# Making the low part of each weight tile one turn later, and moving the last two square-sums of a norm behind the first product of the next opening

## The chip, the cores and the metric

The kernel runs on one core of a Trainium2 chip. The metric is the time on the device, in microseconds (us), as the median of several executions. One execution of the kernel before was also recorded by the hardware profiler, and all rows below come from that one.

## The reference, cut to what matters

Two transformer blocks run one after the other on 512 tokens of width 1024. The first ends in a retrieval layer that picks 16 of 16384 experts for each token and each of 8 heads:

```python
a = jax.nn.gelu(jnp.einsum('tpkd,td->tpk', u[idx], t), approximate=False)
return jnp.einsum('tpk,tpkd->td', (g * a), v[idx])
```

The second block has two layers. Each normalises, mixes (a short convolution or attention, with memory attention beside it), adds, normalises, and runs a gated feed-forward of width 2816:

```python
for i in range(DEPTH_2):
    h = rmsnorm(x, norm_mix[i])
    ...                                   # conv or windowed attention, and memory attention
    x = x + jnp.concatenate([y_tok, y_mem], axis=-1) @ w_out
    h = rmsnorm(x, norm_ffn[i])
    x = x + (jax.nn.silu(h @ w_gate[i]) * (h @ w_up[i])) @ w_down[i]
return rmsnorm(x, final_norm)
```

All of it is float32. The kernel gets that precision from faster matmuls by splitting each operand into a high part and a low part (what the high part leaves over) and adding three products: high by high, low by high, high by low.

## The kernel before, in words

The change touches only the second block. It runs twice, once for each half of the tokens (`half(p, ...)`, p = 0 and 1, 256 tokens each). A half is 184 *products*. A product is one 128-column tile of a weight matrix against the activations: 8 chunks of 128 rows (7 in two thirds of the down projection), and for each chunk three matmuls (`part`, L1813 to L1815). Product n passes through these steps, each in the program of its own engine:

- SyncE loads the raw tile into one of `RAW` = 5 slots once product n-5 is done (`tile`, L1625; it waits for the semaphore `st_used`, which TensorE raises at the end of each product).
- ScalarE copies the high part into one of `SPLIT` = 4 slots once product n-4 is done (`split_hi`, L2150, tile `la_w_hi`; it raises `st_hi`).
- VectorE subtracts the high part from the raw tile and leaves the low part in its place (`split_lo`, L2507, tile `la_w_lo`; it waits for `st_hi` and raises `st_lo`).
- TensorE waits for `st_lo` and for a free PSUM bank (`taken`), and runs the matmuls.
- VectorE, ScalarE or both take the result out of the bank. On VectorE: `scaled` L2520, with `la_work<-la_work` L2609, the product of gate and up, behind each pair of the feed-forward; `add_x` L2527 in the projections back to x. On ScalarE: SiLU L2230, high parts of the hidden L2234, of x L2169, squares L2172. VectorE then makes the low parts: hidden L2594 (`hidden_lo`), x L2512 (`chunk_lo`).

What VectorE does for one product is called a *turn* here. In turn n of the kernel before it takes out product n and then calls `split_lo(n + SPLIT)`.

Each engine's program is a fixed list, and instructions of one engine start in that order. A wait at the head of the list holds everything behind it.

The products of a half come in stages: 20 for the mixing input (the convolution's L2684 to L2693), 8 for `project_out`, 68 for `feed_forward` (22 pairs "in", gate and up, and three groups of 8 "out"), 12 for queries, keys and values, 8 for `project_out`, 68 for `feed_forward`. A stage whose input comes in chunk by chunk begins with an *opening*: three products (`BANKS` = 3) are run on all chunks but the last, and then all three are finished with the last chunk. There are eight openings in a half, among them the last "out" group of each feed-forward.

A norm needs the sum of squares of x over all 8 chunks. ScalarE squares chunk k into one of two slots (L2172, tile `la_sqr`), TensorE adds it up with a matmul by ones (`add_chunk_`, L1849), and after the eighth ScalarE computes the factor `rstd` (`root`, L2159 and L2162). The first five sums stand between the last products of a stage. VectorE needs `rstd` only when it takes out the first product of the next stage.

Beside half 0 the retrieval layer of the first block is still being finished. GpSimd gathers rows of u and v into a ring of 14 slots by indirect DMA (L1694, L1700); VectorE takes dot products of the u rows (`pe_dots`, L2459), TensorE sums the v rows (L1748). The object `beside` spreads this work at some two gathers for each product.

## Time and profile before

| | |
|---|---|
| median of 3 executions | 3271.68 us (3268.64 to 3272.43) |
| the profiled execution | 3267.3 us, of which its span 3265.5 us |
| mean granted clock of TensorE in it | 0.885 of full |
| TensorE matmuls | 2554.1 us busy (78%) |
| VectorE | 1927.5 us (59%) |
| ScalarE | 972.0 us (30%) |
| GpSimd | 1154.3 us (35%) |
| half 0 of the second block, about | 1545 to 2545 us of the span |
| half 1, about | 2545 to 3265 us |

A row of the trace names the engine (PE is TensorE, PEld its weight load, DVE VectorE, ACT ScalarE, POOL GpSimd, SP SyncE), the line, and what is written and read. An arrow `<-` behind an idle time names what ended it. PEclk is the granted clock of TensorE: 1.00 is 2.4 GHz, 0.50 is 1.2 GHz, a value between is a mean over the stretch. The ends of matmuls are modelled, so starts are read and not ends: a matmul shown as 0.28 us long is followed by the next one 0.12 us later.

### The profile page before, as it was taken

To read this page: it belongs to the slowest core of one execution; us is meant where nothing else is said; L and a number is where in the kernel's file an instruction comes from. 1 tells how busy PE (TensorE), PEld (TensorE's weight loads), DVE (VectorE), ACT (ScalarE), POOL (GpSimd) and SP (SyncE) were. 2 spreads that over 40 slices of the span, in tenths; PEclk is the share of its full clock that TensorE was granted. 3 is DMA by queue.
4 is the path that set the end of the run, shared out by engine and by line. 5 is a ranking of instruction groups with operands and counts; after the bars stand their busy time and mean duration, and the time that the engine had idled before them with its cause. 6 is when DMAs were issued, how large, how long until landed. Compare 5 with 4: busy or idle time off the path is not lost.

```text
span 3265.5 us, 43866 instructions
## 1 busy us (share of the span) xinstructions
PE 2554.1 (78%) x16692; PEld 1825.7 (56%) x16692; DVE 1927.5 (59%) x4018; ACT 972.0 (30%) x1693; POOL 1154.3 (35%) x1028
## 2 busy tenths in 40 slices
PE   7887985896056666886757887768999889889898
PEld 4765774554011111222746776526787789876798
DVE  3222766388866666777776776663544655554554
ACT  4443655311000000001223233324333544444433
POOL 0000000066877777777453654474551000000000
PEclk8898997998578889999868999858999999987899
DMA  6222111188899999999887999898996345531353
GB/s 260 94 107 80 47 41 72 44 316 335 288 365 353 363 367 362 392 394 370 298 276 271 365 398 365 324 344 300 402 407 256 117 142 160 164 123 65 118 174 128
DMA packets 218945, 803.92 MB, mean 246 GB/s; under 512 B 24432, under 2 KB 27760, under 8 KB 214768
## 3 DMA queue, kind: packets, MB, share of 16 engines
q0 software_dynamic: 147456, 536.94, 44.0%
q1 hardware_dynamic: 71280, 264.19, 22.7%
q8 instruction: 133, 2.18, 0.3%
q14 instruction: 76, 0.62, 0.1%
HBM read 798.93 MB, written 2.10 MB: 245 GB/s over the span
## 4 chain that ended last, share of the span: by engine, by line
PE 25%; DVE 23%; DMA 10%; issue 10%; ACT 7%; POOL 5%; DVEq 0%; POOLq 0%; ACTq 0%; SPq 0%
DVE la_w_lo L2507 8%; DVE pe_ring L2459 7%; ACT la_w_hi L2150 6%; DMA pe_ring<-in_v,pe_vidx 6%; PE ps L1748 5%; PE ps L1813 5%; PE ps L1814 5%; PE ps L1815 5%; POOL pe_ring L1694 3%; DMA pe_ring<-in_u,pe_idx 2%; POOL pe_ring L1700 2%; PE ps L1711 2%; DVE la_work L2520 1%; DMA la_w_raw<-in_up 1%; PE ps L1879 1%
## 5 line engine op out<-in xcount | busy, mean ns | idle before, releaser
L1694 POOL DMA_INDIRECT pe_ring<-in_u,pe_idx x512 | 601.9, 1176 | 1016.7 <-DVE pe_idxf L2445 655.3
L2459 DVE CUSTOM_DVE_ANT_0 pe_ring<-pe_ring,pe_htok 128x1024 f32<-128x1024 f32 x512 | 613.9, 1222 | 232.9 <-DMA pe_ring<-in_u,pe_idx 226.2
L2507 DVE TENSOR_TENSOR la_w_lo<-la_w_raw,la_w_hi 128x1024 fp32r<-128x1024 f32 (+1 forms) x368 | 442.1, 1202 | 495.9 <-ACT la_w_hi L2150 495.1
L1748 PE MATMUL ps<-pe_ring,pe_spot 128*32 128x512 f32 x2048 | 580.4, 655 | 193.5 <-DMA pe_ring<-in_v,pe_vidx 191.8
L1700 POOL DMA_INDIRECT pe_ring<-in_v,pe_vidx x512 | 552.2, 1078 | 306.6 <-issue 130.5
L1813 PE MATMUL ps<-la_h_hi,la_w_hi 128*128 128x256 f32 x1856 | 544.9, 294 | 48.3 <-DVE la_work L2520 25.6
L1815 PE MATMUL ps<-la_h_hi,la_w_lo 128*128 128x256 f32 x1856 | 533.9, 288 | 0.0
L1814 PE MATMUL ps<-la_h_lo,la_w_hi 128*128 128x256 f32 x1856 | 533.3, 287 | 0.0
L1748 PEld LDWEIGHTS ps<-pe_ring,pe_spot 128*32 128x32 f32 x2048 | 123.5, 115 | 591.4 <-DMA pe_ring<-in_v,pe_vidx 320.8
L2150 ACT ACTIVATE la_w_hi<-la_w_raw 128x1024 fp32r<-128x1024 f32 (+1 forms) x368 | 377.4, 1029 | 216.4 <-DMA la_w_raw<-in_down 56.6
L1813 PEld LDWEIGHTS ps<-la_h_hi,la_w_hi 128*128 128x128 f32 x1856 | 361.1, 195 | 87.7 <-issue 68.9
L1814 PEld LDWEIGHTS ps<-la_h_lo,la_w_hi 128*128 128x128 f32 x1856 | 360.4, 194 | 0.7
L1815 PEld LDWEIGHTS ps<-la_h_hi,la_w_lo 128*128 128x128 f32 x1856 | 359.7, 194 | 0.0
L1813 PE MATMUL ps<-la_b_hi,la_w_hi 128*128 128x256 f32 x1024 | 308.7, 301 | 55.8 <-DVE la_b_lo L2594 39.9
L1814 PE MATMUL ps<-la_b_lo,la_w_hi 128*128 128x256 f32 x1024 | 299.1, 292 | 0.0
L1815 PE MATMUL ps<-la_b_hi,la_w_lo 128*128 128x256 f32 x1024 | 298.7, 292 | 0.0
L1813 PEld LDWEIGHTS ps<-la_b_hi,la_w_hi 128*128 128x128 f32 x1024 | 204.3, 199 | 82.1 <-DVE la_b_lo L2594 42.2
L1814 PEld LDWEIGHTS ps<-la_b_lo,la_w_hi 128*128 128x128 f32 x1024 | 204.5, 200 | 0.4
L1815 PEld LDWEIGHTS ps<-la_b_hi,la_w_lo 128*128 128x128 f32 x1024 | 203.6, 199 | 0.0
L322 PE MATMUL ps<-fr_x_hi,fr_w_hi 128*128 128x512 f32 x256 | 109.0, 426 | 31.0 <-DVE fr_w_lo L181 10.5
L2089 ACT ACTIVATE pe_soft<-pe_soft 128x32 f32<-128x32 f32 (+1 forms) x17 | 3.9, 227 | 417.5 <-DVE pe_soft L2423 417.5
L1711 PE MATMUL ps<-hT,wring 128*128 128x512 f32 x256 | 114.8, 607 | 12.1 <-PEq L250 12.1
(340 smaller groups left out, 3253.5 us busy)
## 6 DMA issues: line engine op xcount, KB each, us to landing
la_w_raw<-in_gate SPq DMA_DIRECT2D x88, 512.0 KB, 4.2
la_w_raw<-in_up SPq DMA_DIRECT2D x88, 512.0 KB, 4.3
la_w_raw<-in_down SPq DMA_DIRECT2D x64, 448.0 KB, 3.8
la_w_raw<-in_a_in SPq DMA_DIRECT2D x40, 512.0 KB, 4.4
wring<-in_w_in SPq DMA_DIRECT2D x32, 512.0 KB, 3.9
la_w_raw<-in_down SPq DMA_DIRECT2D x32, 512.0 KB, 3.7
xT<-in_w_mod SPq DMA_DIRECT2D x8, 1024.0 KB, 4.8
hT<-in_w_mod SPq DMA_DIRECT2D x8, 1024.0 KB, 4.8
```

Source lines behind the costliest of these rows:

```text
L322: pe.matmul(bank, w_hi[:, u, k, :], hi[:, k, :], start=k == 0, stop=False)
L1694: pool.indirect_dma_start(ring[:, n % RING, :], None, io["u"], bass.IndirectOffsetOnAxis(idx[:, t, j:j + 1], 0)).then_inc(land[n % RING], 16)
L1700: pool.indirect_dma_start(ring[:, n % RING, :], None, io["v"], bass.IndirectOffsetOnAxis(vidx[:, t % 2, at:at + 1], 0)).then_inc(land[n % ...
L1711: mm = pe.matmul(ps[:, 4 + side, :], wslot[:, u, k, :], hT[:, k, :], start=k == 0, stop=k == KC - 1)
L1748: return pe.matmul(ps[PER * grp:PER * grp + PER, half, :], spot[:, j // TOKENS % 2, grp, lo:lo + PER], ring[:, n % RING, half * 512:(half ...
L1813: pe.matmul(slot(n), parts_hi[:, n % SPLIT, i, :], hi[:, k, :], start=first, stop=False)
L1814: pe.matmul(slot(n), parts_hi[:, n % SPLIT, i, :], lo[:, k, :], start=False, stop=False)
L1815: return pe.matmul(slot(n), w_lo[:, n % RAW, i, :], hi[:, k, :], start=False, stop=last)
L1879: mm = pe.matmul(score_bank(p, u)[:, b * HT + blocks[0] * P:(b + 1) * HT], q[rows, tt * P:(tt + 1) * P], keys, start=True, stop=True)
L2150: act.activation(parts_hi[:, n % SPLIT, 0:nk, :], raw(n, nk), ACT.Copy).then_inc(st_hi, 1)
L2459: dve.tensor_tensor_reduce(ring[:, n % RING, :], ring[:, n % RING, :], htok[:, t, :], 1.0, 0.0, ALU.mult, ALU.add, dots[:, t % 2, j:j + 1] ...
L2507: dve.tensor_tensor(w_lo[:, n % RAW, 0:nk, :], raw(n, nk), parts_hi[:, n % SPLIT, 0:nk, :].bitcast(F32), ALU.subtract).then_inc(st_lo, 1)
```

## The change

Two edits, both in the order of the instructions; none is added or removed.

First, in turn n VectorE calls `split_lo(n + SPLIT - 1)` in place of `split_lo(n + SPLIT)`, everywhere, and before the first turn it prepares three tiles and not four.

Second, the sums of the last two squares of a norm (chunks 6 and 7) move from the end of the stage to behind the first product of the next opening, in the three norms of each half that are followed by an opening (two before a feed-forward, one before the queries). For the last norm of a half they stay where they were.

```diff
-    NORMS = 5
+    NORMS, BEFORE_LAST = 5, KC - 2
...
                         part(n + u, i, chunks[i], hi, lo, at == 0, False)
+                    if u == begun[0] and sums is not None:
+                        last_sums(sums)
                 arrived(len(order) - 1)
...
+            def last_sums(norm):
+                for k in range(BEFORE_LAST, KC):
+                    add_chunk_(norm, k)
...
-                for k in range(KC - BANKS, KC):
+                for k in range(KC - BANKS, BEFORE_LAST):
                     add_chunk_(p * NORMS + 2 + 2 * layer, k)
...
+                last_sums(p * NORMS + 4)
...
                         scaled(p, n, g_ff[:, which % 2, :])
-                        split_lo(n + SPLIT)
+                        split_lo(n + SPLIT - 1)
                         if pending is not None:
                             hidden_lo(pending)
...
                         dve.tensor_tensor(hid_ff[:, which % 2, :], silu_ff[:, which % 2, :], up_ff[:, which % 2, :], ALU.mult).then_inc(hid_done, 1)
-                        split_lo(n + 1 + SPLIT)
+                        split_lo(n + SPLIT)
                         pending = which
...
                     add_x(p, n, j)
-                    split_lo(n + SPLIT)
+                    split_lo(n + SPLIT - 1)
...
-                    for u in range(SPLIT):
+                    for u in range(SPLIT - 1):
                         split_lo(u)
```

On TensorE, where half 1 goes from its second `project_out` (operands `la_b_hi`, `la_b_lo`) to the feed-forward (`la_h_hi`, `la_h_lo`), the kernel before has these rows. `hg_rooted` is here the semaphore of the low parts of h.

```order
L1815 MATMUL ps<-la_b_hi,la_w_lo 128x256
L1849 MATMUL ps<-la_sqr,const 128x256 [waits la_sq_done] x4
L1813 MATMUL ps<-la_h_hi,la_w_hi 128x256 [waits hg_rooted,st_free0,st_lo]
L1814 MATMUL ps<-la_h_lo,la_w_hi 128x256
L1815 MATMUL ps<-la_h_hi,la_w_lo 128x256
L1813 MATMUL ps<-la_h_hi,la_w_hi 128x256 [waits hg_rooted]
```

In the changed kernel the same place reads:

```order
L1815 MATMUL ps<-la_b_hi,la_w_lo 128x256
L1851 MATMUL ps<-la_sqr,const 128x256 [waits la_sq_done] x2
L1813 MATMUL ps<-la_h_hi,la_w_hi 128x256 [waits hg_rooted,st_free0,st_lo]
L1814 MATMUL ps<-la_h_lo,la_w_hi 128x256
L1815 MATMUL ps<-la_h_hi,la_w_lo 128x256
L1813 MATMUL ps<-la_h_hi,la_w_hi 128x256 [waits hg_rooted]
```

Seven chunks later, where the second product of the opening begins, it has the other two sums:

```order
L1813 MATMUL ps<-la_h_hi,la_w_hi 128x256 [waits hg_rooted]
L1814 MATMUL ps<-la_h_lo,la_w_hi 128x256
L1815 MATMUL ps<-la_h_hi,la_w_lo 128x256
L1851 MATMUL ps<-la_sqr,const 128x256 [waits la_sq_done] x2
L1813 MATMUL ps<-la_h_hi,la_w_hi 128x256 [waits st_free1,st_lo]
```

Two of the four sums stand now behind 21 matmuls of the next stage, which wait only for the low parts of h.

On VectorE the order of kinds is the same through the middle of the program, since each turn still makes one low part, only that of another tile. It shows at both ends. Ahead of half 0 the kernel before has:

```order
L2459 ISA pe_dots 128x1
L2507 TENSOR_TENSOR la_w_lo<-la_w_raw,la_w_hi 128x1024 [waits st_hi] x4
L2655 SCALAR_TENSOR_TENSOR xT<-xT,const,rstd 128x256 [waits la_rooted]
L2655 SCALAR_TENSOR_TENSOR xT<-xT,const,rstd 128x256
L2512 SCALAR_TENSOR_TENSOR la_h_lo<-xT,const,la_h_hi 128x256 [waits hg_head_done]
```

The changed kernel has three low parts there:

```order
L2466 ISA pe_dots 128x1
L2514 TENSOR_TENSOR la_w_lo<-la_w_raw,la_w_hi 128x1024 [waits st_hi] x3
L2662 SCALAR_TENSOR_TENSOR xT<-xT,const,rstd 128x256 [waits la_rooted]
L2662 SCALAR_TENSOR_TENSOR xT<-xT,const,rstd 128x256
L2519 SCALAR_TENSOR_TENSOR la_h_lo<-xT,const,la_h_hi 128x256 [waits hg_head_done]
```

At the end of half 1, in the last eight turns of the last "out" group, the kernel before ends so on VectorE:

```order
L2527 TENSOR_TENSOR xT<-ps,xT 128x256 [waits st_used]
L2507 TENSOR_TENSOR la_w_lo<-la_w_raw,la_w_hi 128x1024 [waits st_hi]
L2527 TENSOR_TENSOR xT<-ps,xT 128x256 [waits st_used] x4
L2738 SCALAR_TENSOR_TENSOR la_work<-xT,const,rstd 128x256 [waits la_rooted]
L2738 SCALAR_TENSOR_TENSOR la_work<-xT,const,rstd 128x256 x7
```

And the changed one:

```order
L2534 TENSOR_TENSOR xT<-ps,xT 128x256 [waits st_used]
L2514 TENSOR_TENSOR la_w_lo<-la_w_raw,la_w_hi 128x1024 [waits st_hi]
L2534 TENSOR_TENSOR xT<-ps,xT 128x256 [waits st_used] x3
L2745 SCALAR_TENSOR_TENSOR la_work<-xT,const,rstd 128x256 [waits la_rooted]
L2745 SCALAR_TENSOR_TENSOR la_work<-xT,const,rstd 128x256 x7
```

The last tile's low part is made with three turns left to take out and not four: one turn later, as everywhere between.

## Rows read from the trace of the kernel before

**Rows 1.** The page: chain that ended last; costliest groups on VectorE and ScalarE
```profile
DVE la_w_lo L2507 8%; DVE pe_ring L2459 7%; ACT la_w_hi L2150 6%; DMA pe_ring<-in_v,pe_vidx 6%; PE ps L1748 5%; PE ps L1813 5%; PE ps L1814 5%; PE ps L1815 5%; POOL pe_ring L1694 3%; DMA pe_ring<-in_u,pe_idx 2%; POOL pe_ring L1700 2%; PE ps L1711 2%; DVE la_work L2520 1%; DMA la_w_raw<-in_up 1%; PE ps L1879 1%
...
L2507 DVE TENSOR_TENSOR la_w_lo<-la_w_raw,la_w_hi 128x1024 fp32r<-128x1024 f32 (+1 forms) x368 | 442.1, 1202 | 495.9 <-ACT la_w_hi L2150 495.1
...
la_w_raw<-in_gate SPq DMA_DIRECT2D x88, 512.0 KB, 4.2
```

**Rows 2.** Busy time by stretch: stretch, length, PE PEld DVE ACT POOL, PEclk, DMA, GB/s
```profile
1560.00:1757.00 197.00, 121.77 (x755) 108.97 (x754) 148.32 (x263) 49.55 (x87) 87.33 (x76) 0.75 0.81 278
1757.30:2040.60 283.30, 242.22 (x1868) 210.13 (x1866) 195.20 (x314) 90.16 (x132) 147.45 (x134) 0.95 0.96 366
2080.00:2266.00 186.00, 138.87 (x781) 78.21 (x779) 102.95 (x242) 55.67 (x151) 120.02 (x106) 0.73 0.94 351
2340.00:2400.00 60.00, 60.00 (x495) 47.40 (x495) 27.07 (x39) 20.12 (x27) 32.69 (x31) 1.00 1.03 408
2663.10:2885.00 221.90, 203.45 (x1595) 199.85 (x1594) 120.19 (x182) 89.08 (x126) 0.00 (x0) 0.95 0.50 162
3034.90:3255.00 220.10, 203.31 (x1598) 200.64 (x1596) 118.22 (x179) 86.36 (x120) 0.00 (x0) 0.95 0.46 146
```

**Rows 3.** Timeline, half 1, feed-forward: one pair on VectorE and ScalarE
```profile
2697.41 0.43 DVE L2609 TENSOR_TENSOR la_work<-la_work 128x256 f32<-128x256 f32 x1
2697.87 0.42 ACT L2234 ACTIVATE la_b_hi<-la_work 128x256 fp32r<-128x256 f32 x1 [2.49 <-DVE la_work L2609]
2698.19 1.05 ACT L2150 ACTIVATE la_w_hi<-la_w_raw 128x1024 fp32r<-128x1024 f32 x1
2699.27 1.23 DVE L2507 TENSOR_TENSOR la_w_lo<-la_w_raw,la_w_hi 128x1024 fp32r<-128x1024 f32 x1 [1.44 <-ACT la_w_hi L2150]
2700.42 0.42 DVE L2520 TENSOR_TENSOR la_work<-ps,rstd 128x256 f32<-128x256 f32 x1
2700.87 0.42 ACT L2230 ACTIVATE la_work<-la_work 128x256 f32<-128x256 f32 x1 [1.62 <-DVE la_work L2520]
...
2702.27 1.23 DVE L2507 TENSOR_TENSOR la_w_lo<-la_w_raw,la_w_hi 128x1024 fp32r<-128x1024 f32 x1 [1.43 <-ACT la_w_hi L2150]
2703.41 0.42 DVE L2594 TENSOR_TENSOR la_b_lo<-la_work,la_b_hi 128x256 fp32r<-128x256 f32 x1
...
2704.26 0.42 DVE L2609 TENSOR_TENSOR la_work<-la_work 128x256 f32<-128x256 f32 x1
```

**Rows 4.** Timeline, TensorE in the feed-forward of half 1: two L1813, nine matmuls apart
```profile
3120.09 0.28 PE L1813 MATMUL ps<-la_h_hi,la_w_hi 128*128 128x256 f32 x1
...
3121.16 0.28 PE L1813 MATMUL ps<-la_h_hi,la_w_hi 128*128 128x256 f32 x1
```

**Rows 5.** Waits in 3010 to 3265 us: waiting, for what, us, times, longest
```profile
PE ps L1813 <- DVE la_b_lo L2594: 12.9, 3, 4.8
```

**Rows 6.** Busy time by stretches of 5 us, half 1
```profile
3030.00:3035.00 5.00, 2.03 (x5) 1.22 (x5) 1.96 (x3) 2.98 (x6) 0.00 (x0) 0.50 0.00 0
...
3070.00:3075.00 5.00, 4.28 (x36) 4.07 (x35) 2.32 (x3) 2.58 (x4) 0.00 (x0) 1.00 0.61 209
```

**Rows 7.** Timeline, half 1, from `project_out` to the feed-forward
```profile
3026.62 0.70 PE L1849 MATMUL ps<-la_sqr,const 128*128 128x256 f32 x2 [1.00 <-ACT la_sqr L2172]
...
3030.41 1.22 PE L1849 MATMUL ps<-la_sqr,const 128*128 128x256 f32 x2 [3.08 <-ACT la_sqr L2172]
...
3034.19 1.22 PE L1849 MATMUL ps<-la_sqr,const 128*128 128x256 f32 x2 [2.56 <-ACT la_sqr L2172]
3034.85 0.78 PE L1813 MATMUL ps<-la_h_hi,la_w_hi 128*128 128x256 f32 x1
...
3038.18 0.42 ACT L2162 ACTIVATE rstd<-rstd 128x256 f32<-128x256 f32 x1
```

**Rows 8.** Timeline, half 0, the same place: a sum, a dot product
```profile
1753.01 1.22 DVE L2459 CUSTOM_DVE_ANT_0 pe_ring<-pe_ring,pe_htok 128x1024 f32<-128x1024 f32 x1
...
1756.62 1.22 PE L1849 MATMUL ps<-la_sqr,const 128*128 128x256 f32 x2 [4.86 <-ACT la_sqr L2172]
```

**Rows 9.** Waits in 1758 to 2040 us (first feed-forward of half 0)
```profile
DVE la_w_lo L2507 <- ACT la_w_hi L2150: 81.2, 57, 1.9
...
POOL pe_ring L1694 <- DVE pe_dots L2459: 49.4, 14, 5.6
```

More of the change, by code:

```diff
@@ L1824, in product, with opening @@
                 mm.then_inc(st_used, 1)
-            def opening(n, hi, lo, beside, arrived, order=None, chunks=range(KC), held=None):
+            def opening(n, hi, lo, beside, arrived, order=None, chunks=range(KC), held=None, sums=None):
                 order = order if order is not None else range(len(chunks))
@@ L1941, in feed_forward @@
                 b = b_chunks(p, 1 + 2 * layer)
-                opening(n, h_hi, h_lo, beside, lambda at: pe.wait_ge(h_lo_in, h_chunks(p, 1 + 2 * layer) + at + 1))
+                opening(n, h_hi, h_lo, beside, lambda at: pe.wait_ge(h_lo_in, h_chunks(p, 1 + 2 * layer) + at + 1), sums=p * NORMS + 1 + 2 * layer)
                 begin = n + BANKS
@@ L1970, in project_out @@
                     add_chunk_(p * NORMS + 1 + 2 * block_, j - BANKS)
-                for k in range(KC - BANKS, KC):
+                for k in range(KC - BANKS, BEFORE_LAST):
                     add_chunk_(p * NORMS + 1 + 2 * block_, k)
@@ L1995, in half @@
                 n += N_FF
-                opening(n, h_hi, h_lo, beside, lambda at: pe.wait_ge(h_lo_in, h_chunks(p, 2) + at + 1))
+                opening(n, h_hi, h_lo, beside, lambda at: pe.wait_ge(h_lo_in, h_chunks(p, 2) + at + 1), sums=p * NORMS + 2)
                 steps, first = attention(p, 1, n), True
@@ L2631, in project_out @@
                     add_x(p, n, j)
-                    split_lo(n + SPLIT)
+                    split_lo(n + SPLIT - 1)
                     n += 1
@@ L2664, in half @@
                     scaled(p, n, q_of(pr), DH ** -0.5)
-                    split_lo(n + SPLIT)
+                    split_lo(n + SPLIT - 1)
                     n += 1
@@ L2675, in half @@
                     beside()
-                    split_lo(n + SPLIT)
+                    split_lo(n + SPLIT - 1)
                     if i:
@@ L2693, in half @@
                     late(dve.scalar_tensor_tensor(taps_cv[:, 0, :], gated[:, 2:HT + 2], tap[2], taps_cv[:, 1, :], ALU.mult, ALU.add))
-                    split_lo(n + 1 + SPLIT)
+                    split_lo(n + SPLIT)
                     if p and i:
@@ L2700, in half @@
                     dve.tensor_tensor(out_cv[:, i % 2, :], taps_cv[:, 0, :], y_cv[:, 0, :], ALU.mult).then_inc(cv_made, 1)
-                    split_lo(n + 2 + SPLIT)
+                    split_lo(n + SPLIT + 1)
                     n += 3
@@ L2717, in half @@
                         scaled(p, n, kT[:, which, p * HT:(p + 1) * HT] if kind == "k" else v_raws[p][:, which, :])
-                    split_lo(n + SPLIT)
+                    split_lo(n + SPLIT - 1)
                     n += 1
```

## The prediction

> **What bounds the kernel now.** I read the page first. Its chain of work that ended last spends 8% of the span in VectorE's low parts of weight tiles and 6% in ScalarE's high parts, more than in any one matmul line, and the group of the 368 low parts stands idle 495.1 us in all, waiting for ScalarE [rows 1]. The question is whether TensorE feels that.
>
> The busy time by stretch answers it stage by stage [rows 2]. In the two feed-forwards of half 1 TensorE is busy 203 of 222 and 203 of 220 us, at a mean clock of 0.95, VectorE about 120, ScalarE under 90, DMA half used. In the second feed-forward of half 0 (2340 to 2400) TensorE has 60.00 of 60 us at full clock and DMA moves 408 GB/s with a share of 1.03: that stage is full. The first part of half 0 has neither: 278 GB/s in 1560 to 1757, 366 in 1757 to 2041.
>
> The timeline of one pair of the feed-forward shows what limits half 1 [rows 3]. VectorE and ScalarE take turns: ScalarE's high part (1.05 us) starts only when VectorE has delivered; VectorE, standing at the low part of the same tile, waits 1.44 us for it, works 1.23, takes out the next product (0.42), and only then ScalarE goes on. From one L2609 to the next it is 2704.26 - 2697.41 = 6.85 us a pair. TensorE needs less: nine matmuls take 3121.16 - 3120.09 = 1.07 us, 0.119 each [rows 4], so 48 of a pair take 5.71 us. The pair is late by 1.14 us each time; TensorE runs ahead on its free banks and then stops. It stops for lack of a bank (4.28 of 5 us busy in 3070 to 3075 [rows 6]) and where a group of "out" needs the hidden part that the ring has not made: three stops of 4.3 us, up to 4.8, in this stretch [rows 5].
>
> At the change of stage the same ring has three steps more. The pairs of sums come 3034.19 - 3030.41 = 3.78 us apart, with TensorE waiting 1.00, 3.08 and 2.56 us for squares [rows 7]; meanwhile the clock falls to 0.50 [rows 6]. In half 0, with two dot products (1.22 each) in a turn, that wait is 4.86 us [rows 8].
>
> **The first edit, the low part one turn later.** In turn n VectorE then asks for tile n+3, whose high part was released when product n-1 ended, a whole product earlier. The wait of 1.4 us goes in nearly every turn, and the two engines overlap. VectorE's work for a pair is 2 x 1.23 + 4 x 0.42 = 4.14 us, ScalarE's 2 x 1.05 + 2 x 0.42 = 2.94, both under TensorE's 5.71: TensorE becomes the bound.
>
> Half 1, feed-forwards. 1595 and 1598 matmuls at 0.119 us are 189.8 and 190.2 us [rows 2, 4] against 221.9 and 220.1: 32.1 + 29.9 = 62.0 us are lost now, by idling and by the half clock behind each stop. I leave 4 us in each (a wait named below, and the sums, which are slower than split matmuls), and take -54. Lower bound: if the ring only shrinks to a smaller one, half of it, -27; upper bound, all 62.
>
> New cost of the edit. After an opening three products end almost together: behind product n come two last chunks, 2 x 3 x 0.119 = 0.71 us, and then TensorE wants the low part of n+3. It was ready before; now it is made in turn n, 0.42 + 1.23 = 1.65 us after product n. TensorE waits 0.94 us. Queued behind that wait are all later products. There are 16 openings: 15 us, of which I charge 8 in half 1 (4 of them within the 8 left above, so +4 here) and +4 in half 0, where most are covered by rows of v summed there. In the steady state the low part is ready 1.65 us after product n and wanted after two products, 5.7 us: 4 us to spare, and the deepest turn of half 0, with two dot products ahead, needs 1.65 + 2.44 = 4.1. A waiting raw tile lands 4.2 us after issue [rows 1] with four products for it, so loads stay hidden. Nothing hides the 0.94 us in half 1.
>
> Half 1 elsewhere. In the products between sums the turn shrinks from 3.78 us to TensorE's 24 x 0.119 + 0.36 for a sum = 3.22: 5 x 0.56 = 2.8 for each of two `project_out`, -5. The mixing and attention stages are chains of their own; I take -2 there (bounds 0 and -10).
>
> Half 0. VectorE waits 81.2 us for high parts within the 283 us of the first feed-forward, and GpSimd's gathers wait behind its dot products, 49.4 us for u alone [rows 9]. After the edit the limit there is DMA: 283.3 x 366 / 408 = 254 us [rows 2]. The ring of slots has to fill first, so I take 263, -20 (bounds 0 and -29). In 1560 to 1757 VectorE is busy 148 of 197 us, and in the middle stages its dot products and convolution are a real load: -8, and for `project_out`, whose turns shrink by the 1.3 us that the wait for ScalarE lasts there, 5 x 1.3 = -6. The attention stretch (2080 to 2266, DMA 0.94) and the second feed-forward (full) give nothing.
>
> Here the Trainium skill speaks against me: "DMA: Bandwidth & Descriptors", section "Where 436 GB/s comes from", takes about 358 GB/s as what binds a transfer from HBM to SBUF. By it the 366 GB/s of that stretch would already be the limit and half 0 would give nothing in it. The 408 GB/s of 2340 to 2400 contradict the figure on this core, and the sum goes by that row; the case without the gain is the first rival.
>
> **The second edit, two sums behind the first product.** Half 1 has three such places. From the end of the last product (3026.62 minus the 1.00 of waiting, so 3025.6) to the first matmul of the opening (3034.85) it is 9.2 us [rows 7]; the other two are the same code with the same turns, and I take 9 for each from this one, 27. Of this the four sums are 4 x 0.36 = 1.4 us. Afterwards the first product's chunks need only low parts of h. With the ring gone, chunk 6 is there about 0.42 + 1.23 + 0.48 = 2.1 us after the last product, and TensorE comes to it after two sums and six chunks, 0.7 + 2.1 = 2.8 us. Chunk 7's square is ready by then. So -(27 - 4) = -23, and -2 for the opening of the queries, which no longer runs at half clock (the others are in the stretches above). The norm's factor comes later relative to the opening: sums done at 0.7 + 2.5 + 0.7 = 3.9 us, and 3038.18 + 0.42 - 3035.1 = 3.5 us for the root, so 7.4; the first product of the opening ends at 0.7 + 7.5 + 0.7 + 0.4 = 9.3. It hides, with 1.9 us to spare; without that, each us late would be one us at six places.
>
> Half 0 has three places too. The one at 2266 has no dot products: -7. At the other two a turn still holds two dot products, 4.6 us of VectorE against some 4 of TensorE, so the low parts of h come later than TensorE wants them: I take -6 each of about 10, -12.
>
> Of the clock: behind the stops for squares it stands at 0.50 in 3030 to 3035, while the short stops of 3070 to 3075, 0.72 us in 5, leave it at 1.00 [rows 6]. I count on the new 0.94 us waits to leave it too. "TensorE: Matmul & The Clock Gate" of the Trainium skill, section "A second HAM failure mode: psum-queue depth-cycling", says that short idles between groups of matmuls can be frequent enough to throttle. The trace of this stretch does not show it; it is a rival below.
>
> **The sum.** Half 1: -54 + 4 - 5 - 2 - 23 - 2 = -82. Half 0: -20 - 8 - 6 + 4 - 7 - 12 = -49, which I cut to -39, because what is won in one stretch of half 0 partly only moves gathers into the stretches where DMA is at 0.94 or more. Together -121: 3267.3 - 121 = 3146 for the profiled execution. The median of the runs is 4.4 us above that execution: 3151.
>
> **The rivals.**
> 1. *DMA takes half 0.* The gathers bound half 0 whatever VectorE does; only half 1's 82 us come: 3190. For it: shares of 0.94 to 0.96 in 1757 to 2266 [rows 2]. Against it: 366 and 351 GB/s are under 408, and GpSimd waits for dot products [rows 9].
> 2. *A smaller ring in place of the old.* ScalarE's hidden high part still needs VectorE's product of gate and up, and VectorE's next turn needs SiLU. If these keep the engines in step, about half is won, -60: 3212. Against it: 4.14 and 2.94 us of work in 5.71.
> 3. *Slower: the lead is gone.* TensorE may now be only three products ahead of VectorE's low parts, not four. If the old lag of VectorE is not caused by the wait but by the length of its turns, TensorE stops for low parts at each of the 16 openings and falls to the half clock: 0.94 us of waiting and some 2 us at 0.50 behind it, 16 x 3 = 48 us: 3320. It decides as soon as VectorE is over 4 us behind. Against it: VectorE is busy 120 of 220 us.
> 4. *Short waits drop the clock,* with everything else as forecast: 16 x 2 us back, 3183.
> 5. *The order does not matter,* since the end is set elsewhere: 3272. Against it, the three stops for hidden parts.
>
> **How the numbers follow.** Forecast 0.70; rival 1, 0.13; rival 2, 0.07; rival 3, 0.04; rival 4, 0.03; rival 5, 0.03. What a measurement of this kernel can tell from no change is about 0.2%, 6.5 us. Rivals 1, 2 and 4 are faster too, so faster 0.93, same 0.03, slower 0.04. The range: at the low end half 1 gives 92 (all 62 of its feed-forwards) and half 0 some 68 (its uncut 49 and the outer bounds of its stretches): 3112. At the high end half 1 gives 60 and half 0 nothing: 3212, which takes in rivals 1, 2 and 4.
>
> **What would show it.** In the changed profile the idle time in front of the low parts should fall from 495 us to under 200, most of what is left in the stage where DMA is full. A pair in half 1 should come every 5.7 to 5.8 us, the waits for hidden parts and for squares should be gone from TensorE, and PEclk in both feed-forwards of half 1 should be 0.99 or 1.00. A new wait of about 1 us for the low part should stand behind each opening. In 1760 to 2020 DMA should move over 390 GB/s. I am wrong if a pair still takes over 6.3 us, if the low part is what TensorE waits for within a stage, or if the first feed-forward of half 0 keeps its 283 us.

## The result, and the profile after

| | before | after |
|---|---|---|
| median of 4 executions | 3272.05 us (3268.64 to 3275.49) | 3108.11 us (3099.67 to 3123.71) |
| profiled execution, span | 3267.3, 3265.5 us | 3115.5, 3113.7 us |
| granted clock | 0.885 | 0.898 |
| TensorE busy | 2554.1 us (78%) | 2512.3 us (81%) |

The ratio is 0.9499 by the medians, 0.9504 [0.9459, 0.9549] by all runs: 164 us faster. The forecast was 121 us faster, 3151, with a range down to 3112. The sign and the mechanism were right, the size too small by a quarter. Line numbers of the changed kernel are up to 7 higher: L1813 stays, L1849 is L1851, L2150 is L2157, L2507 is L2514, L2609 is L2616.

The page of the changed kernel, first the chain, then the group of low parts:

```profile
PE 37%; DVE 13%; DMA 12%; issue 9%; POOL 6%; ACT 1%; POOLq 0%; DVEq 0%; ACTq 0%; SPq 0%
PE ps L1813 9%; DMA pe_ring<-in_v,pe_vidx 9%; PE ps L1815 8%; PE ps L1814 8%; PE ps L1748 7%; DVE pe_ring L2466 6%; POOL pe_ring L1694 3%; POOL pe_ring L1700 3%; DMA pe_ring<-in_u,pe_idx 3%; DVE la_w_lo L2514 2%; PE ps L1711 2%; PE ps L1885 1%; PE ps L1851 1%; PE ps L1911 1%; PE ps L1894 1%
...
L2514 DVE TENSOR_TENSOR la_w_lo<-la_w_raw,la_w_hi 128x1024 fp32r<-128x1024 f32 (+1 forms) x368 | 440.5, 1198 | 91.1 <-ACT la_w_hi L2157 89.3
```

The low parts had 8% of the chain [rows 1] and have 2%. The idle time in front of them fell from 495.9 to 91.1 us, while their busy time stayed (442.1, 440.5). The matmuls and the DMA took their place in the chain.

For the stages I cut both traces at the same event, the start of the step that computes `rstd` for the feed-forward or for the queries, and at the first and the last norm of a half. The second edit moves that event: it starts 1.55 us behind the first matmul of the opening before, and 4.5 us behind it after (8.6 and 5.4 us at the first two places of half 0). The last column cuts at the first matmul of the opening instead; the sums over a half are the same:

| us | before | after | difference | opening to opening |
|---|---|---|---|---|
| half 0: mixing input, attention, `project_out` | 197.9 | 173.0 | -24.9 | -32.0 |
| half 0: first feed-forward | 295.0 | 263.7 | -31.3 | -28.2 |
| half 0: queries to second `project_out` | 214.8 | 204.1 | -10.7 | -9.8 |
| half 0: second feed-forward | 274.3 | 263.4 | -10.9 | -8.0 |
| half 1: mixing input, `project_out` | 107.2 | 100.3 | -6.9 | -9.8 |
| half 1: first feed-forward | 230.8 | 196.7 | -34.1 | -34.2 |
| half 1: queries to second `project_out` | 141.1 | 127.3 | -13.8 | -13.8 |
| half 1: second feed-forward | 220.8 | 194.3 | -26.5 | -23.4 |

Half 0 gave 77.8 us (forecast 39) and half 1 81.3 (forecast 82). The work before half 0, which the change does not touch, took some 7 us longer in this execution; the sum is then the 152 us by which the two profiled executions differ, and the other 12 us to the medians are the spread of executions (this one is 7.4 us above its median, that of before 4.7 below).

The windows behind four of these rows, before and then after (columns as in [rows 2]):

```profile
1758.82:2053.84 295.02, 244.83 (x1874) 211.53 (x1873) 202.55 (x327) 94.40 (x138) 151.78 (x137) 0.94 0.95 362
2268.60:2542.92 274.32, 264.50 (x2124) 214.95 (x2123) 125.95 (x198) 95.83 (x134) 113.50 (x106) 0.98 0.85 330
2664.48:2895.33 230.85, 206.35 (x1602) 201.38 (x1601) 124.09 (x189) 93.99 (x133) 0.00 (x0) 0.94 0.49 158
3036.40:3257.17 220.77, 203.29 (x1596) 199.83 (x1594) 116.94 (x178) 87.01 (x121) 0.00 (x0) 0.95 0.45 146
```

```profile
1741.08:2004.74 263.66, 241.34 (x1874) 206.68 (x1874) 200.78 (x326) 97.15 (x138) 161.12 (x137) 0.95 1.01 398
2208.87:2472.23 263.36, 258.65 (x2107) 209.34 (x2105) 127.22 (x196) 97.35 (x134) 111.38 (x106) 1.00 0.90 348
2587.02:2783.76 196.74, 194.27 (x1602) 193.23 (x1601) 123.45 (x188) 94.78 (x133) 0.00 (x0) 1.00 0.57 185
2911.03:3105.38 194.35, 191.72 (x1579) 190.09 (x1577) 117.11 (x177) 87.63 (x122) 0.00 (x0) 1.00 0.52 166
```

In both feed-forwards of half 1 TensorE is now busy all but 2.5 and 2.6 us, at a granted clock of 1.00, full speed; it had been 0.94 and 0.95. The first feed-forward of half 0 moves 398 GB/s with a DMA share of 1.01: that stage is now full.

One pair of the feed-forward of half 1 on VectorE, the answer to [rows 3]:

```profile
2718.78 0.43 DVE L2616 TENSOR_TENSOR la_work<-la_work 128x256 f32<-128x256 f32 x1
...
2719.12 1.22 DVE L2514 TENSOR_TENSOR la_w_lo<-la_w_raw,la_w_hi 128x1024 fp32r<-128x1024 f32 x1
2721.13 0.42 DVE L2527 TENSOR_TENSOR la_work<-ps,rstd 128x256 f32<-128x256 f32 x1 [0.79 <-PE ps L1815]
2721.47 1.22 DVE L2514 TENSOR_TENSOR la_w_lo<-la_w_raw,la_w_hi 128x1024 fp32r<-128x1024 f32 x1
2722.60 0.42 DVE L2601 TENSOR_TENSOR la_b_lo<-la_work,la_b_hi 128x256 fp32r<-128x256 f32 x1
2724.01 0.42 DVE L2527 TENSOR_TENSOR la_work<-ps,rstd 128x256 f32<-128x256 f32 x1 [0.99 <-PE ps L1815]
2724.53 0.43 DVE L2616 TENSOR_TENSOR la_work<-la_work 128x256 f32<-128x256 f32 x1
```

The pair takes 2724.53 - 2718.78 = 5.75 us and not 6.85. No low part waits for ScalarE; VectorE now waits for TensorE's products instead, 0.79 and 0.99 us. The arrow has turned round: TensorE is the bound.

What stood on TensorE at that place before was this, in six pairs in a row of each feed-forward:

```profile
3072.52 0.39 PE L1813 MATMUL ps<-la_h_hi,la_w_hi 128*128 128x256 f32 x1 [0.72 <-DVE la_w_lo L2507]
```

It is the idle time of the stretch 3070 to 3075 that the forecast put down to a missing bank. The trace puts it down to the low part, which is what the ring makes late.

The waits of TensorE in half 1, all of its lines:

```profile
PE ps L1813 <- DVE la_w_lo L2514: 7.8, 8, 1.0
PE ps L1894 <- DVE pe_ring L2568: 5.0, 5, 1.9
PE ps L1813 <- DVE la_h_lo L2519: 1.6, 3, 0.5
PE ps L1813 <- DVE la_b_lo L2730: 0.3, 1, 0.3
```

The stops for hidden parts (three in [rows 5], six in the whole half) and the waits for squares [rows 7] are gone. For low parts of weights TensorE waits eight times, 0.93 to 1.02 us, once behind each of the eight openings; the forecast had 0.94 us and eight of them. The kernel before waited 8.0 us for them too, but at another place: 13 times up to 0.7 us, in the pairs.

### The profile page after: what moved, and what is told of

Same layout as the page of the kernel before. It is cut to its first block, busy times and chain, and to the rows that moved or that the text cites. A ratio compares the mean times of both kernels' runs of the same rounds, so it can differ in the third digit from the quotient of the medians.

```text
span 3113.7 us, 43866 instructions
## 1 busy us (share of the span) xinstructions
PE 2512.3 (81%) x16692; PEld 1796.8 (58%) x16692; DVE 1924.0 (62%) x4018; ACT 977.9 (31%) x1693; POOL 1153.2 (37%) x1028
## 4 chain that ended last, share of the span: by engine, by line
PE 37%; DVE 13%; DMA 12%; issue 9%; POOL 6%; ACT 1%; POOLq 0%; DVEq 0%; ACTq 0%; SPq 0%
PE ps L1813 9%; DMA pe_ring<-in_v,pe_vidx 9%; PE ps L1815 8%; PE ps L1814 8%; PE ps L1748 7%; DVE pe_ring L2466 6%; POOL pe_ring L1694 3%; POOL pe_ring L1700 3%; DMA pe_ring<-in_u,pe_idx 3%; DVE la_w_lo L2514 2%; PE ps L1711 2%; PE ps L1885 1%; PE ps L1851 1%; PE ps L1911 1%; PE ps L1894 1%
## 5 line engine op out<-in xcount | busy, mean ns | idle before, releaser
L1813 PE MATMUL ps<-la_h_hi,la_w_hi 128*128 128x256 f32 x1856 | 536.5, 289 | 27.0 <-DVE la_w_lo L2514 19.7
L2514 DVE TENSOR_TENSOR la_w_lo<-la_w_raw,la_w_hi 128x1024 fp32r<-128x1024 f32 (+1 forms) x368 | 440.5, 1198 | 91.1 <-ACT la_w_hi L2157 89.3
L2157 ACT ACTIVATE la_w_hi<-la_w_raw 128x1024 fp32r<-128x1024 f32 (+1 forms) x368 | 379.5, 1034 | 336.2 <-DMA la_w_raw<-in_down 104.2
L1813 PEld LDWEIGHTS ps<-la_h_hi,la_w_hi 128*128 128x128 f32 x1856 | 353.9, 191 | 63.5 <-DVE la_w_lo L2514 37.6
L1814 PEld LDWEIGHTS ps<-la_h_lo,la_w_hi 128*128 128x128 f32 x1856 | 353.6, 191 | 0.5
L1813 PE MATMUL ps<-la_b_hi,la_w_hi 128*128 128x256 f32 x1024 | 299.6, 293 | 9.0 <-DVE la_w_lo L2514 5.6
L1815 PE MATMUL ps<-la_b_hi,la_w_lo 128*128 128x256 f32 x1024 | 291.7, 285 | 0.0
L1814 PE MATMUL ps<-la_b_lo,la_w_hi 128*128 128x256 f32 x1024 | 291.2, 284 | 0.0
L1813 PEld LDWEIGHTS ps<-la_b_hi,la_w_hi 128*128 128x128 f32 x1024 | 196.0, 191 | 32.0 <-issue 13.8
L1814 PEld LDWEIGHTS ps<-la_b_lo,la_w_hi 128*128 128x128 f32 x1024 | 195.6, 191 | 0.6
L1815 PEld LDWEIGHTS ps<-la_b_hi,la_w_lo 128*128 128x128 f32 x1024 | 195.3, 191 | 0.0
L2527 DVE TENSOR_TENSOR la_work<-ps,rstd 128x256 f32<-128x256 f32 x190 | 80.4, 423 | 174.5 <-PE ps L1815 174.4
```

The source lines that it names most:

```text
L1813: pe.matmul(slot(n), parts_hi[:, n % SPLIT, i, :], hi[:, k, :], start=first, stop=False)
L1814: pe.matmul(slot(n), parts_hi[:, n % SPLIT, i, :], lo[:, k, :], start=False, stop=False)
L1815: return pe.matmul(slot(n), w_lo[:, n % RAW, i, :], hi[:, k, :], start=False, stop=last)
L2157: act.activation(parts_hi[:, n % SPLIT, 0:nk, :], raw(n, nk), ACT.Copy).then_inc(st_hi, 1)
L2514: dve.tensor_tensor(w_lo[:, n % RAW, 0:nk, :], raw(n, nk), parts_hi[:, n % SPLIT, 0:nk, :].bitcast(F32), ALU.subtract).then_inc(st_lo, 1)
L2527: dve.tensor_tensor(dst, slot(n), r, ALU.mult).then_inc(freed(n), 1)
```

## The experiments

Ten kernels were run in three groups, two of them twice, each group on one chip with its own runs of the kernel before. In the first group that kernel took 3275.01 us; in the second and third, which share another chip, 3363.76 and 3367.36. So ratios are compared across chips, and microseconds inside one. Medians are of 6 executions, of 12 for sums_only and of 2 for the two kernels named nov. The traces give half 0 and half 1 of the second block apart (sums of four stages cut as above):

| kernel | median, us | ratio [95%] | half 0 | half 1 |
|---|---|---|---|---|
| changed kernel, group 1 | 3107.33 | 0.9492 [0.9457, 0.9527] | 905.6 | 620.4 |
| low_only | 3109.55 | 0.9506 [0.9478, 0.9534] | 902.1 | 620.8 |
| two_late | 3112.07 | 0.9512 [0.9483, 0.9541] | 901.7 | 624.5 |
| early_fourth | 3091.67 | 0.9451 [0.9418, 0.9485] | 896.4 | 611.7 |
| sums_only, group 2 | 3361.43 | 0.9983 [0.9954, 1.0012] | 996.6 | 702.1 |
| low_late_half1 | 3283.99 | 0.9741 [0.9699, 0.9782] | 1005.2 | 617.3 |
| before_nov | 3322.25 | 0.9858 [0.9798, 0.9917] | 956.7 | 699.9 |
| after_nov | 3145.19 | 0.9332 [0.9272, 0.9392] | 852.2 | 620.2 |
| changed kernel, group 3 | 3199.35 | 0.9502 [0.9464, 0.9540] | 922.4 | 610.7 |
| changes_late | 3249.42 | 0.9649 [0.9604, 0.9694] | 959.4 | 618.6 |
| fourth_no_sums | 3195.66 | 0.9498 [0.9461, 0.9536] | 912.1 | 614.1 |
| early_fourth_again | 3197.91 | 0.9497 [0.9459, 0.9535] | 922.2 | 611.8 |

The kernel before has 982.0 and 699.9 on the chip of the first profile.

### Which of the two edits does it: low_only and sums_only

low_only has the first edit alone, sums_only the second alone:

```diff
 # low_only, against the changed kernel
-                for k in range(KC - BANKS, BEFORE_LAST):
+                for k in range(KC - BANKS, KC):
...
-                    if u == begun[0] and sums is not None:
-                        last_sums(sums)
 # sums_only, against the changed kernel
-                        split_lo(n + SPLIT - 1)
+                        split_lo(n + SPLIT)
```

> Only the first edit: the low part of each weight tile one turn later; all eight sums of a norm stay ahead of the opening. Theory A (the ring between VectorE and ScalarE was nearly all of it): with the ring gone TensorE waits at a change of stage only for one add (0.42), one high part of x (0.51) and one square (0.40), some 1.3 to 2.5 us, at six places: 8 to 15 us above the changed kernel, 3116 to 3123. Theory B (the split that the prediction made, in which the sums are worth 44 us of the 121): 3145 to 3155.

> Only the second edit: the last two sums behind the opening's first product; low parts at their old place. Theory A (ring): the opening starts two sums earlier, but VectorE is still a turn and a half behind, and the opening's first product stops for the low part of x of chunk 6, or runs at half clock; 1 to 3 us at each of six places: 3254 to 3266. Theory B (the prediction's split, sums worth 44): 3225 to 3230.

> The changed kernel once more, beside the other three on the same chip: 3100 to 3115 us, so that they can be set against it.

The first edit alone gives the whole gain: 3109.55 against 3107.33 us of the changed kernel on the same chip, which is no difference that can be measured, and under both of its theories (8 to 15 us above, or more). The second alone gives 0.9983, an interval that holds 1: 2 us, less than even its first theory gave it (6 to 18). The forecast had put 44 us on the second (23 + 2 in half 1, 7 + 12 in half 0). With the first edit in place there is hardly a wait for squares left to save. In low_only the sums behind the last product begin at 2893.34, and these are the last rows before the opening starts at 2896.43:

```profile
2893.34 1.80 PE L1849 MATMUL ps<-la_sqr,const 128*128 128x256 f32 x6
...
2896.09 0.70 PE L1849 MATMUL ps<-la_sqr,const 128*128 128x256 f32 x2 [0.95 <-ACT la_sqr L2176]
```

That is 3.1 us for four sums. In the kernel before the same four take 9.8 us, from this row to the opening at 3034.85 (the forecast's 9.2 begins behind the first of them):

```profile
3025.03 0.59 PE L1849 MATMUL ps<-la_sqr,const 128*128 128x256 f32 x2
```

One wait of 0.95 us is left in place of 1.00, 3.08 and 2.56. So the ring at the change of stage was the first edit's to remove, and what the second edit could still win, a wait of about 1 us at each place, it partly gives back: the opening of the changed kernel waits 0.53 us for a low part of h.

```profile
2909.50 0.39 PE L1813 MATMUL ps<-la_h_hi,la_w_hi 128*128 128x256 f32 x1 [0.53 <-DVE la_h_lo L2519]
```

Without the first edit the waits only change their name. In half 1 of the kernel before TensorE waits 20.6 us for squares and 8.0 for low parts of weights. In half 1 of sums_only it has these:

```profile
PE ps L1813 <- DVE la_w_lo L2514: 18.4, 16, 6.1
PE ps L1813 <- DVE la_h_lo L2529: 6.0, 2, 3.2
PE ps L1851 <- ACT la_sqr L2179: 3.8, 3, 1.8
```

The opening starts earlier and stops for VectorE instead, and half 1 takes 702.1 us, no less than the 699.9 of before_nov on the same chip.

### How much lead VectorE needs: two_late and early_fourth

two_late makes the low part yet one turn later (tile n+2). early_fourth keeps the changed order and makes one low part more just before each opening, so that none is missing behind it:

```diff
 # two_late
-                        split_lo(n + SPLIT - 1)
+                        split_lo(n + SPLIT - 2)
 # early_fourth, at the end of a stage that an opening follows
+                lows(n + BANKS)      # low parts up to tile n + 3, each made once
```

> The changed kernel with each low part yet one turn later (in turn n the tile n+2; before each opening the low parts of its three products are made). Theory A: TensorE wants the low part of n+3 two products (5.7 us) after product n, and it comes in turn n+1, 2.9 + 0.42 + 1.23 = 4.6 us after it: nothing lost within the stages of half 1, 1 to 2 us behind each opening; in half 0, where a turn takes 4.8 us with its dot products, 6.4 us after it: lost at many products. 15 to 50 us above the changed kernel, nearly all of it in half 0. Theory C (any lead suffices, only the wait for ScalarE matters): under 10 us above.

> The changed kernel, and before each opening VectorE makes one low part more, that of the product behind the opening, while it has nothing else to do; the turns after it make one less until the count is even. The wait of about 1 us on TensorE behind each opening should go. If all 16 openings pay for it: 10 to 15 us under the changed kernel. If most of it is hidden in half 0 (8 openings pay): 6 to 8 us under. If the late low part costs nothing: no difference.

> The changed kernel with one low part more made before each opening, run again beside the changed kernel. If the low parts that the opening waits for are worth what the trace of the changed kernel shows (about 1 us at each of two openings per stage), it lies some 10 to 16 us below the changed kernel, ratio to the kernel before about 0.945. If the first measurement was chance, it lies within 4 us of the changed kernel.

The waits of TensorE for low parts over the whole execution, two_late first, then the changed kernel on the same chip, then early_fourth:

```profile
PE ps L1813 <- DVE la_w_lo L2514: 49.3, 40, 4.3
```

```profile
PE ps L1813 <- DVE la_w_lo L2514: 25.9, 20, 3.1
```

```profile
PE ps L1813 <- DVE la_w_lo L2514: 16.3, 8, 3.1
```

With one more turn of lead given up the waits double, 23 us more, yet half 1 is only 4 us longer, half 0 is not longer at all, and the median is 5 us higher, inside what the intervals leave open. The first theory (15 to 50 us, nearly all in half 0) missed, and "under 10" held. So the third rival ("the lead is gone", 3320) is far off even for a kernel with less lead than it assumed. The page of two_late has a second lesson:

```profile
L2514 DVE TENSOR_TENSOR la_w_lo<-la_w_raw,la_w_hi 128x1024 fp32r<-128x1024 f32 (+1 forms) x368 | 439.1, 1195 | 6.2 <-ACT la_w_hi L2157 5.5
```

The idle time in front of the low parts goes 495.9, 91.1, 6.2 us over the three kernels; the medians of the first group go 3275, 3107, 3112. The last 85 us of idle time brought nothing when they went. That TensorE or the DMA was the bound by then fits this, but no run shows it for those 85 us alone.

early_fourth removes in half 1 what the rows promised; the eight waits that its line shows all stand in half 0. Its stages there are 98.2, 194.3, 127.3 and 191.9 us against 100.3, 196.7, 129.1 and 194.3, and the waits for low parts are gone from them; run again it had 98.2, 194.3, 127.4 and 191.9. That is 7 us in three stages; the fourth, from queries to `project_out`, ran at another clock in one of the traces (last section). Half 0 was 9 us shorter in one trace and equal in the other. The medians say 15.7 us faster than the changed kernel in the first group and 1.4 in the third. The second time is inside the 4 us that its expectation called chance. So by the medians no gain over the changed kernel is shown; the 7 us of half 1 are in both traces, the rest stays open.

### Whether the two halves add up: low_late_half1

```diff
+                lows(n + (4 if n < PRODUCTS else 3))   # half 0 as before, half 1 late
```

> The changed kernel, but in half 0 VectorE makes the low parts at their old place; only half 1 has them one turn later. The two traces say that half 1 gave 81 us and half 0 78. If the halves add up: half 1 as in the changed kernel, half 0 within 15 us of before (the moved sums remain): 3272 - 81 - 5 to 15, 3176 to 3186.

Half 1 takes 617.3 us, as in the changed kernel (610.7 and 620.4), half 0 1005.2, within 9 us of the 996.6 of sums_only. On this chip the kernel before took 3363.76 us: 80 us for half 1 alone. With the 0.9502 of the changed kernel (168 us) some 88 are left for half 0. The halves add up, and half 0 is worth as much as half 1.

### What bounds the first feed-forward of half 0: before_nov and after_nov

Both kernels leave out the gathers of rows of v for all but the first two groups of tokens; in their place stands a small transfer of 8 columns with the same semaphores, so the output is another one. The traffic falls, the order and the waits between the engines stay.

```diff
+                    if t >= 2:
+                        pool.dma_start(ring[:, n % RING, 0:8], io["v"][0:P, 0:8]).then_inc(land[n % RING], 16)
+                        continue
```

> The kernel before without the gathers of v of the last two token tiles (a small transfer of 8 columns stands in for each, and the sums run over what lies in the slot). This takes a third to two thirds of the transfers out of half 0. If the ring of VectorE and ScalarE sets the pace of the first feed-forward of half 0, it keeps its 295 us from norm to norm within 10. If the DMA engines set it, it falls by the bytes, to 240 or less.

> The changed kernel without the same gathers of v. If DMA is what bounds the first feed-forward of half 0 now (398 GB/s on the mean), it falls from 264 us to what TensorE or VectorE need, 225 to 245. If it stays at 264, DMA does not bound it. The second feed-forward, where TensorE is busy all the time, should keep 263 within 5 either way.

The same stage, in before_nov and then in after_nov:

```profile
1839.31:2134.75 295.44, 245.03 (x1874) 212.06 (x1873) 202.26 (x327) 94.28 (x137) 114.10 (x137) 0.94 0.71 240
```

```profile
1831.01:2062.86 231.85, 230.38 (x1874) 202.60 (x1874) 199.95 (x326) 96.44 (x137) 125.76 (x137) 0.99 0.88 306
```

With a third of the traffic gone (240 GB/s, not 362) the old order still takes 295 us (299.7 with all the traffic, in sums_only on the same chip): the gathers of v did not bound that stage, and the first rival falls; that the ring did is what the new order shows. With the new order the stage goes from 263.3 us (changed kernel, group 3) to 231.9 when the traffic goes: now DMA bounds it, and TensorE (230.38 of 231.85 us busy) stands right behind. The second feed-forward keeps 264.9 us with the traffic down to 134 GB/s, as expected. The attention stage loses 34 us with the old order (224.5 in sums_only, 190.8) and 40 with the new one (222.3 in group 3, 182.0), so DMA bound it in part with either.

### Where the gain of half 0 sits: changes_late

Half 1 late throughout; in half 0 only the turns of `project_out` and of the last "out" group of each feed-forward are late, 32 of 184 (the expectation has 192 by mistake). In the first turn of each such group VectorE makes no low part, and behind the last it makes two.

```diff
+                changes = [AT_OUT0, AT_Q - KC, AT_OUT1, PRODUCTS - KC]
+                lows(n + (4 if n < PRODUCTS and not any(at <= n < at + KC for at in changes) else 3))
```

> The changed kernel with the low parts one turn later in all of half 1, but in half 0 only in its turns of project_out and of the last group of each feed-forward (88 to 95, 176 to 183); in every other turn of half 0 the low part stands where it stood before the change. Half 0 gained 78 us in the trace of the changed kernel. Theory B (half 0 gains where stages change, because there the ring of VectorE, ScalarE and TensorE sets the pace, while inside a stage the stream or VectorE sets it): at least 50 of the 78 us come, so this kernel lies at most 25 to 30 us above the changed one, ratio to the kernel before about 0.957 to 0.959. Theory A (the gain is spread evenly over all turns of half 0): 32 of its 192 turns are late, so 15 to 20 of the 78 come, and it lies 55 to 60 us above the changed one, ratio about 0.967.

> The changed kernel once more, for comparison on the same chip: ratio to the kernel before 0.949, with all theories alike; the other three kernels of this call are compared with it.

The result lies between the theories: 50 us above the changed kernel, ratio 0.9649. By medians (low_late_half1 put on this group's scale: 3283.99 x 3367.36 / 3363.76 = 3287.5) the 32 turns bring 38 of 88 us; by the traces 45.8 of 82.8. By stage, in microseconds:

| stage of half 0 | low_late_half1 | changes_late | changed kernel | the late 32 turns | the rest |
|---|---|---|---|---|---|
| mixing input to `project_out` | 201.5 | 183.7 | 172.2 | -17.8 | -11.5 |
| first feed-forward | 299.6 | 286.3 | 263.3 | -13.3 | -23.0 |
| queries to `project_out` | 232.2 | 222.6 | 222.3 | -9.6 | -0.3 |
| second feed-forward | 271.9 | 266.8 | 264.6 | -5.1 | -2.2 |

A sixth of the turns brings about half of the gain. The claim that it all sits at the changes of stage is wrong, and so is the even spread. The rest comes from inside the first feed-forward (23.0) and from ahead of `project_out` (11.5), mostly the convolution: its turns of three products come every 15.3 us before and every 13.8 after, six times. Inside the attention stage and the full feed-forward there is next to nothing.

### The sums once more: fourth_no_sums

early_fourth with the two sums put back to the end of the stage:

```diff
-                for k in range(KC - BANKS, BEFORE_LAST):
+                for k in range(KC - BANKS, KC):
```

> The kernel that makes one low part more before each opening, with the sums of the last two squares put back where they stood before the change (behind the last product). Theory A (with the low part one turn later the place of the sums is worth nothing, as the kernel with the first edit alone showed): within 5 us of the same kernel with the sums moved, ratio to the kernel before 0.944 to 0.947. Theory C (with the opening no longer short of low parts, TensorE's wait for the squares is what is late at a change of stage): about 10 us longer, ratio about 0.948.

3195.66 against 3197.91 us: no difference, as the first theory said, though the ratio of both is above its 0.947, as that of early_fourth_again is. In half 1 the traces differ by 2.3 us (614.1, 611.8) in favour of the moved sums, under 1 us a place. TensorE's waits for squares in its half 1 are three, which is one for each place:

```profile
PE ps L1849 <- ACT la_sqr L2176: 2.9, 3, 1.0
```

## Why the prediction was right and wrong

**Right: the mechanism, and half 1.** The forecast said that asking for a tile whose high part was released one product earlier breaks the ring of VectorE and ScalarE. The pair fell to 5.75 us (forecast 5.7 to 5.8), the idle time to 91 us (under 200), the clock rose to 1.00, the waits for hidden parts and squares went, and half 1 gave 81.3 us against 82. From opening to opening the feed-forwards gave 57.6 us against the 54 of their term, and the rest of the half 23.6 against 28. low_only shows that this 82 was right in sum and wrongly shared out: the 25 us written against the second edit belong to the first. One reading was wrong without harm to the sum: TensorE's stops within the pairs are for low parts, not for a bank.

**Right: the price of the thinner lead, in half 1.** 1.0 us behind each opening against 0.94, no drop of the clock behind it, and none of the three us each that the third rival counted. "TensorE: Matmul & The Clock Gate" of the Trainium skill, section "A second HAM failure mode: psum-queue depth-cycling", tells of a kernel whose short idles between groups of matmuls throttled the clock (the fourth rival). The trace does not bear it out here: the windows of both feed-forwards, each with two such waits, stand at 1.00.

In half 0 one of the forecast's own signs of being wrong came true, that the low part is what TensorE waits for within a stage. There it waits 17.6 us for low parts, where the forecast charged 4 and the kernel before had no such wait; 14 us of it are five waits in the convolution, two of them here:

```profile
1603.29 0.39 PE L1813 MATMUL ps<-la_h_hi,la_w_hi 128*128 128x256 f32 x1 [3.04 <-DVE la_w_lo L2514]
1617.11 0.39 PE L1813 MATMUL ps<-la_h_hi,la_w_hi 128*128 128x256 f32 x1 [3.04 <-DVE la_w_lo L2514]
```

The stage is not slower for it. The kernel before waited there, too, for other results of VectorE, and for this one every 15.35 us where it is now every 13.82:

```profile
1598.44 0.36 PE L1813 MATMUL ps<-la_h_hi,la_w_hi 128*128 128x256 f32 x1 [2.02 <-DVE la_work L2684]
1613.79 0.55 PE L1813 MATMUL ps<-la_h_hi,la_w_hi 128*128 128x256 f32 x1 [3.34 <-DVE la_work L2684]
```

The 1.5 us between the two are the wait for ScalarE's high part that VectorE no longer has; what is left of its turns is its own work, without a gap in the trace. There VectorE is the bound, and TensorE's waits for low parts say so. The price of the lead in half 0 was not measured apart.

**Wrong: half 0, 39 forecast and 77.8 measured.** Four steps failed.

1. *The cut from 49 to 39*, "because what is won in one stretch of half 0 partly only moves gathers into the stretches where DMA is at 0.94 or more". No stage of half 0 got longer. The gathers of v did not bound the first feed-forward before (before_nov: 295 us without them, 300 with them in sums_only), and where they did in part, in the attention stage, 10 us were won all the same. The first stage has only 8 gathers of v, and no run here leaves out gathers of u, so that case stays open.

2. *"For `project_out`, whose turns shrink by the 1.3 us that the wait for ScalarE lasts there, 5 x 1.3 = -6."* This is the largest error for its length. One turn there, before:

```profile
1739.32 1.22 DVE L2507 TENSOR_TENSOR la_w_lo<-la_w_raw,la_w_hi 128x1024 fp32r<-128x1024 f32 x1 [1.83 <-ACT la_w_hi L2150]
1740.46 0.48 DVE L2512 SCALAR_TENSOR_TENSOR la_h_lo<-xT,const,la_h_hi 128x256 fp32r<-128x256 f32 x1
1740.86 1.22 DVE L2459 CUSTOM_DVE_ANT_0 pe_ring<-pe_ring,pe_htok 128x1024 f32<-128x1024 f32 x1
...
1743.15 0.42 DVE L2527 TENSOR_TENSOR xT<-ps,xT 128x256 f32<-128x256 f32 x1
...
1745.40 1.22 DVE L2507 TENSOR_TENSOR la_w_lo<-la_w_raw,la_w_hi 128x1024 fp32r<-128x1024 f32 x1 [1.83 <-ACT la_w_hi L2150]
```

and after:

```profile
1728.33 1.24 DVE L2514 TENSOR_TENSOR la_w_lo<-la_w_raw,la_w_hi 128x1024 fp32r<-128x1024 f32 x1
1729.46 0.50 DVE L2519 SCALAR_TENSOR_TENSOR la_h_lo<-xT,const,la_h_hi 128x256 fp32r<-128x256 f32 x1
1729.86 1.24 DVE L2466 CUSTOM_DVE_ANT_0 pe_ring<-pe_ring,pe_htok 128x1024 f32<-128x1024 f32 x1
...
1732.14 0.44 DVE L2534 TENSOR_TENSOR xT<-ps,xT 128x256 f32<-128x256 f32 x1
1732.48 1.24 DVE L2514 TENSOR_TENSOR la_w_lo<-la_w_raw,la_w_hi 128x1024 fp32r<-128x1024 f32 x1
```

The ring was 6.08 us a turn, with 1.83 us in which VectorE waits for the three ScalarE steps in series (0.51, 0.40, 1.04); after it is 4.15 us, and VectorE never idles. That is 1.93 us a turn and it holds in all eight turns: 15 us, not 6. The forecast put the wait at 1.3, for which its rows show no source, and counted only the five turns between the sums. The last "out" group has the same turns, with chunks of x made beside them, and was given nothing of its own. Summed up, the four changes of stage in half 0 were charged 6 + 7 + 12 = 25 us, less 4 for the openings; changes_late measured 38 to 46, all of it from the first edit.

3. *"The ring of slots has to fill first, so I take 263, -20."* It did not have to fill: the stage went to the rate that DMA can move. From one `rstd` step to the next the limit is 295.0 x 362 / 408 = 262 us, and it took 263.7. The outer bound of that term, -29, was nearly the result: from opening to opening it is -28. Here "DMA: Bandwidth & Descriptors" of the Trainium skill, section "Where 436 GB/s comes from", has about 358 GB/s as what binds such a transfer; the stage ran at 398, and the forecast that set it aside for the measured 408 was right to.

4. *"The second feed-forward (full) gives nothing."* The row for this was one stretch of 60 us in its middle [rows 2], and for the middle it is true (-2.2 us inside). As a whole the stage had 264.50 of 274.32 us busy at a clock of 0.98; its last group and its start were not full, and from its opening on it gave 8.0.

With the steps put right from what the runs show, half 0 is 37 us inside the stages (23 + 12 and 2 elsewhere) and 38 to 46 at the changes, where the uncut forecast had 28 and 21. Both were too small, and the second is where most of the time was missed. The range ended at 3112 because its low end took 68 us for half 0. Its own terms with the outer bound of the feed-forward give only 49 + 9 = 58, and half 0 gave 77.8.

**The rivals.** DMA takes half 0: refuted by before_nov for the first feed-forward, and by the 77.8 us that half 0 gave. A smaller ring: refuted by the pair of 5.75 us. The lead is gone: refuted by two_late. Short waits drop the clock: refuted by the 1.00 of the feed-forwards of half 1. The order does not matter: refuted by low_only.

## What to carry to other kernels

Where two in-order engines hand tiles to each other, ask of each item how long its producer has been free to start it when the consumer stands at it; if that is nothing, moving the request one turn later costs no work and ends the ring, and the lead that is given up cost here about 1 us where three products end together. Price a ring turn by turn at each place with its own steps in series, the rare turns first: here a sixth of the turns of half 0 held half of its gain, and a wait read in one stage was no measure for another. A stage is "full" only from its first to its last turn, never by a stretch in its middle; and two edits aimed at the same idle time are not to be charged one after the other before asking what the first leaves.

## What the runs showed of the hardware

The same kernel took 3275.01 us on one chip and 3363.76 on another (17 runs, 3348.36 to 3390.50), 2.7% apart, while the changed kernel's ratio held: 0.9492 and 0.9502. The one other kernel that ran on both, early_fourth, had 0.9451 and 0.9497, and their intervals overlap. The traces put nearly all of it ahead of half 0, whose first norm came at 1542 to 1546 us in the first group and at 1610 to 1643 in the others, and some 16 us into the attention stage of half 0 (206.4 and 222.3 us in the changed kernel); the feed-forwards of half 1 agree to 0.1 us.

The granted clock of one stage differed between executions of one kernel. The stage from queries to `project_out` in half 1 had these windows in the changed kernel, first profile and third group:

```profile
2783.76:2911.03 127.27, 118.41 (x758) 92.38 (x757) 69.55 (x176) 66.94 (x162) 0.00 (x0) 0.87 0.25 83
```

```profile
2870.14:2989.58 119.44, 107.55 (x758) 86.86 (x757) 69.50 (x176) 66.92 (x161) 0.00 (x0) 0.96 0.27 89
```

The same 758 matmuls took 118.41 us at 0.87 and 107.55 at 0.96: 8 us of the span with the same instructions, which is more than several of the effects looked for here. In the nine other traces with low parts one or two turns late in half 1 the stage stood at 0.84 to 0.88. What decides it between executions was not found.
